# The gated embedding of a two-block transformer forward pass: its product moved to third place in the stream, its gates applied pair by pair, the next stage's chunk splits begun beside it, and the output stored in four parts

## The reference

```python
def swiglu_2(x, wg, wu, wd):
    return (jax.nn.silu(x @ wg) * (x @ wu)) @ wd

for i in range(DEPTH):                       # DEPTH = 2
    x = layer_norm(DN_ALPHA * x + 0.5 * swiglu_2(x, ffn1_wg[i], ffn1_wu[i], ffn1_wd[i]), ...)
    y = mixer_ab(x, ...) if i % 2 == 0 else mixer_c(x, ...)
    x = layer_norm(DN_ALPHA * x + y, ...)
    x = layer_norm(DN_ALPHA * x + 0.5 * swiglu_2(x, ffn2_wg[i], ffn2_wu[i], ffn2_wd[i]), ...)
    x = x + jax.nn.sigmoid(x @ ple_wg[i] + ple_bg[i]) * (p[i] @ ple_wp[i])
return x
```

## Time and profile before

| | |
|---|---|
| median of 3 runs | 2382.51 us |
| the three runs | 2378.83, 2382.51, 2384.23 us |
| profiled execution | 2382.22 us |
| its span in the profile | 2380.4 us |
| TensorE matmuls busy | 2220.4 us (93%) |
| VectorE, ScalarE busy | 1377.1 us (58%), 941.4 us (40%) |
| mean granted clock | 0.967 |

### The profile page before, as it was taken

The page is one execution under the profiler, slowest core; times in us unless marked ns, Lnnn a source line. Parts: engine busy times, 40 slices in busy tenths (PEclk is TensorE's granted clock), DMA queues, the critical chain, the costliest instruction groups (busy, mean ns, idle before and its releaser), DMA issues. The chain is left out here.

```text
span 2380.4 us, 32569 instructions
## 1 busy us (share of the span) xinstructions
PE 2220.4 (93%) x13722; PEld 1897.6 (80%) x13722; DVE 1377.1 (58%) x1600; ACT 941.4 (40%) x1031; POOL 127.0 (5%) x69
## 2 busy tenths in 40 slices
PE   6999889999999978999999979999799998789997
PEld 4887678888888747888888868888788796678886
DVE  4458724756665164666656655655565695636654
ACT  3313323545443143444444443444344444124443
POOL 0056300000000000000000000000000020000000
PEclk8999999999999999999999989999899998899999
DMA  7228804455455301555555414554355442024551
GB/s 313 106 105 358 351 1 152 172 184 182 171 192 182 112 17 71 194 189 183 190 181 193 160 53 150 186 194 159 124 193 182 153 176 73 2 76 154 186 194 54
DMA packets 52481, 373.10 MB, mean 157 GB/s; under 512 B 5728, under 2 KB 6752, under 8 KB 7840
## 3 DMA queue, kind: packets, MB, share of 16 engines
q1 hardware_dynamic: 51584, 367.78, 42.1%
q0 software_dynamic: 800, 3.93, 0.5%
HBM read 370.64 MB, written 1.05 MB: 156 GB/s over the span
## 5 line engine op out<-in xcount | busy, mean ns | idle before, releaser
L359 PE MATMUL PS<-AR_r 128*128 128x512 f32 x2240 | 792.9, 398 | 0.0
L479 DVE TENSOR_TENSOR ring_r<-ring,AR_r 128x2048 fp32r<-128x2048 f32 x270 | 619.1, 2299 | 277.2 <-ACT AR_r L473 277.1
L473 ACT ACTIVATE AR_r<-ring 128x2048 fp32r<-128x2048 f32 x274 | 522.4, 1912 | 315.8 <-PE PS L376 194.0
L360 PE MATMUL PS<-AR_r,ring_r 128*128 128x256 f32 x2240 | 628.2, 280 | 0.0
L359 PEld LDWEIGHTS PS<-AR_r 128*128 128x128 f32 x2240 | 420.8, 188 | 103.1
L360 PEld LDWEIGHTS PS<-AR_r,ring_r 128*128 128x128 f32 x2240 | 422.8, 189 | 2.5
L531 ACT ACTIVATE AR<-PS 128x512 f32<-128x512 f32 x140 | 83.8, 599 | 439.3 <-PE PS L360 439.3
L374 PE MATMUL PS<-AR_r 128*128 128x512 f32 x616 | 242.1, 393 | 0.0
L376 PE MATMUL PS<-AR_r 128*128 128x512 f32 x616 | 240.9, 391 | 0.0
L375 PE MATMUL PS<-ring_r,AR_r 128*128 128x512 f32 x616 | 240.1, 390 | 0.0
L376 PEld LDWEIGHTS PS<-AR_r 128*128 128x128 f32 x616 | 115.6, 188 | 26.3
(11 more groups left out here) (377 smaller groups left out, 3070.2 us busy)
## 6 DMA issues: line engine op xcount, KB each, us to landing
ring<-stream SPq DMA_DIRECT2D x346, 1024.0 KB, 4.8
X<-xt SPq DMA_DIRECT2D x1, 2048.0 KB, 10.1
AR<-bias POOLq DMA_DIRECT2D x1, 1536.0 KB, 6.7
AR<-pt POOLq DMA_DIRECT2D x2, 512.0 KB, 4.3
out<-X SPq DMA_DIRECT2D x1, 1024.0 KB, 4.8
SM<-small SPq DMA_DIRECT2D x1, 545.0 KB, 4.2
AR<-invc SPq DMA_DIRECT2D x1, 512.0 KB, 15.3
X<-negl POOLq DMA_DIRECT2D x1, 512.0 KB, 6.4
```

The source lines that it names most:

```text
L359: pe.matmul(PS[:, bank, :], w_hi, X_PARTS[:, :, k * T:(k + 1) * T], start=(k == 0), stop=False, skip_group_check=True)
L360: ins = pe.matmul(PS[:, bank, 0:T], w_lo, X_HI[:, k, :], start=False, stop=(k == DT - 1), skip_group_check=True)
L473: act.activation(w_hi_of(tag, i), ring[:, n % SLOTS, :], ACT.Identity).then_inc(split_hi, 1)
L479: dve.tensor_tensor(RING_R[:, n % SLOTS, :], ring[:, n % SLOTS, :], w_hi_of(tag, i), ALU.subtract).then_inc(split_lo, 1)
```

## The change

The embedding's chunk becomes a stage of its own (`emb2`, `emb3`) between the first two and the last two gate chunks (`ple2b`, `ple3b`), in the stream and in TensorE's order. VectorE applies pairs 0 and 1 as soon as the embedding's product and their gates are there, pair 2 behind the third chunk's gates, pair 3 behind the fourth's. For layer 2, the splits of ffn4's chunks 0 and 1 are placed between these steps on both engines, and the input's first pair is rounded before the last two gates are taken. ScalarE gets a wait on the last product before that rounding, since `X_HI` is still read until then. The places of the rounded chunks turn differently (`TURN_OF`), and the waits that free them are given by `free`. The output is stored in four transfers, each behind its pair's `ple_out`.

```diff
-          ("ffn2", FF_CHUNKS), ("mix2_in", 7), ("mix2_out", 4), ("ffn3", FF_CHUNKS), ("ple2", 5),
-          ("ffn4", FF_CHUNKS), ("mix3_in", 16), ("mix3_out", 4), ("ffn5", FF_CHUNKS), ("ple3", 5)]
+          ("ffn2", FF_CHUNKS), ("mix2_in", 7), ("mix2_out", 4), ("ffn3", FF_CHUNKS), ("ple2", 2), ("emb2", 1), ("ple2b", 2),
+          ("ffn4", FF_CHUNKS), ("mix3_in", 16), ("mix3_out", 4), ("ffn5", FF_CHUNKS), ("ple3", 2), ("emb3", 1), ("ple3b", 2)]
...
-        TURN_OF = {"ffn1_lat": 2, "ffn2": 2, "mix2_in": 2}
+        TURN_OF = {"ple2b": 2, "ple3b": 2, "ffn4": 1, "mix3_in": 1, "ffn1_lat": 2, "ffn2": 2, "mix2_in": 2}
...
-            act_split_chunk(act, nxt, 2)
+            if nxt.startswith("ple"):
+                act_split_chunk(act, f"{nxt}b", 0, free=START[nxt])
+            else:
+                act_split_chunk(act, nxt, 2)
...
         def pe_ple(pe, l):
-            n0 = START[f"ple{l}"]
             pe_chunks_as_features_come(pe, f"ple{l}", (0, 1), (0, 1))
-            for i in range(2, 4):
-                pe_chunk_split(pe, f"ple{l}", i, i)
-            need_chunk(pe, n0 + 4)
+            n = START[f"emb{l}"]
+            need_chunk(pe, n)
             pe.wait_ge(S["emb_loaded"], S.at("emb_loaded", l))
...
             ins.then_inc(multiplied, 1)
+            for i in range(2):
+                pe_chunk_split(pe, f"ple{l}b", i, 2 + i)
 
         def act_ple(act, order, l):
-            act_split_chunk(act, f"ple{l}", 3)
-            for m in range(DT):
-                need_product(act, START[f"ple{l}"] + m // 2)
-                b = (l - 2) * 8 + m
-                act.activation(SQ[:, m, LAT], ACC[:, m, :], ACT.Sigmoid, bias=sm("ple_bg")[:, b:b + 1]).then_inc(S["ple_gate"], S.mark("ple_gate", (l, m)))
+            first, then = START[f"ple{l}"], START[f"ple{l}b"]
+
+            def gates(q):
+                need_product(act, first + q if q < 2 else then + q - 2)
+                for m in (2 * q, 2 * q + 1):
+                    b = (l - 2) * 8 + m
+                    act.activation(SQ[:, m, LAT], ACC[:, m, :], ACT.Sigmoid, bias=sm("ple_bg")[:, b:b + 1]).then_inc(S["ple_gate"], S.mark("ple_gate", (l, m)))
+
+            def round_up(q):
+                act.wait_ge(S["ple_out"], S.at("ple_out", (l, q)))
+                act.activation(X_HI[:, pair(q), :], XL[:, pair(q), :], ACT.Identity).then_inc(S["x_hi"], S.mark("x_hi", ("ffn4", q)))
+
+            act_split_chunk(act, f"ple{l}b", 1, free=first + 2)
+            for q in range(2):
+                gates(q)
+            if l == 2:
+                act_split_chunk(act, "ffn4", 0, free=first + 2)
+            gates(2)
+            if l == 2:
+                act_split_chunk(act, "ffn4", 1, free=then + 1)
+                act.wait_ge(multiplied, START["ffn4"])
+                round_up(0)
+            gates(3)
+            if l == 2:
+                for q in range(1, GROUPS):
+                    round_up(q)
+                act_split_chunk(act, "ffn4", 2, free=START["ffn4"])
 
         def dve_ple(dve, order, l):
-            dve_split_chunk(dve, f"ple{l}", 3)
-            need_product(dve, START[f"ple{l}"] + 4)
-            dve.wait_ge(S["ple_gate"], S.at("ple_gate", (l, DT - 1)))
             emb = PS[:, 4:8, :].rearrange("p b (m t) -> p (b m) t", t=T)
-            for q in range(GROUPS):
+
+            def add(q):
+                dve.wait_ge(S["ple_gate"], S.at("ple_gate", (l, 2 * q + 1)))
                 dve.tensor_tensor(SQ[:, pair(q), LAT], SQ[:, pair(q), LAT], emb[:, pair(q)], ALU.mult).then_inc(order.sem, order.step())
                 dve.wait_ge(order.sem, order.n)
                 dve.tensor_tensor(XL[:, pair(q)], XL[:, pair(q)], SQ[:, pair(q), LAT], ALU.add).then_inc(S["ple_out"], S.mark("ple_out", (l, q)))
+
+            dve_split_chunk(dve, f"ple{l}b", 1)
+            need_product(dve, START[f"emb{l}"])
+            for q in range(2):
+                add(q)
+            if l == 2:
+                dve_split_chunk(dve, "ffn4", 0)
+            add(2)
+            if l == 2:
+                dve_split_chunk(dve, "ffn4", 1)
+                dve_split_input(dve, "ffn4", XL, (0,))
+            add(3)
+            if l == 2:
+                dve_split_input(dve, "ffn4", XL, (1, 2, 3))
+                dve_split_chunk(dve, "ffn4", 2)
...
-                if l == 3:
-                    dve_split_first(dve, "ffn4")
-                    dve_split_input(dve, "ffn4", XL)
...
-            sp.wait_ge(S["finished"], S.at("finished"))
...
-                sp.dma_start(out, X[:, :, LAT]).then_inc(S["stored"], S.mark("stored", by=16))
+                for q in range(GROUPS):
+                    sp.wait_ge(S["ple_out"], S.at("ple_out", (3, q)))
+                    sp.dma_start(out[:, pair(q), :], XL[:, pair(q), :]).then_inc(S["stored"], S.mark("stored", by=16))
+                sp.wait_ge(S["finished"], S.at("finished"))
...
-                if l == 3:
-                    act_split_first(act, "ffn4")
-                    act_split_input(act, "ffn4", XL, 0, ("ple_out", 2))
```

More of the change, by code:

```diff
@@ L154, in build @@
                 SPLIT_BASE[name] = chunks
-                chunks += 4 if name.startswith("ple") else count
+                chunks += count
         def arena(at, *shape, of=AR):
@@ L1412, in dve_layernorm @@
                     dve_split_input(dve, nxt, XL, (q - 1,))
-            dve_split_chunk(dve, nxt, 2)
+            if nxt.startswith("ple"):
+                dve_split_chunk(dve, f"{nxt}b", 0)
+            else:
+                dve_split_chunk(dve, nxt, 2)
         PEMB = arena(20736, 2, 2, T)
         def pe_ple(pe, l):
-            n0 = START[f"ple{l}"]
             pe_chunks_as_features_come(pe, f"ple{l}", (0, 1), (0, 1))
-            for i in range(2, 4):
-                pe_chunk_split(pe, f"ple{l}", i, i)
-            need_chunk(pe, n0 + 4)
+            n = START[f"emb{l}"]
+            need_chunk(pe, n)
             pe.wait_ge(S["emb_loaded"], S.at("emb_loaded", l))
@@ L1426, in pe_ple @@
                     ins = pe.matmul(PS[:, 4 + m // 2, (m % 2) * T:(m % 2 + 1) * T],
-                                    ring[:, (n0 + 4) % SLOTS, k * D + m * P:k * D + (m + 1) * P], PEMB[:, l - 2, k, :],
+                                    ring[:, n % SLOTS, k * D + m * P:k * D + (m + 1) * P], PEMB[:, l - 2, k, :],
                                     start=(k == 0), stop=(k == 1))
             ins.then_inc(multiplied, 1)
+            for i in range(2):
+                pe_chunk_split(pe, f"ple{l}b", i, 2 + i)
@@ L2092, in build @@
         AFTER = {"mix0": "mix0_out", "layer0": "ffn0_ctx", "mix1": "mix1_out", "layer1": "ffn1_lat", "preffn2": "ffn2",
-                 "mix2": "mix2_out", "layer2": "ple2", "preffn3": "ffn4", "mix3": "mix3_out", "layer3": "ple3"}
+                 "mix2": "mix2_out", "layer2": "ple2b", "preffn3": "ffn4", "mix3": "mix3_out", "layer3": "ple3b"}
         LASTUSE = START[AFTER[stop or "layer3"]] + dict(STAGES)[AFTER[stop or "layer3"]]
@@ L2476, in lay_out @@
         wp = g["ple_wp_2"][l].reshape(2, P, D).transpose(1, 0, 2).reshape(1, P, -1)
-        parts[f"ple{2 + l}"] = np.concatenate([chunks_in(g["ple_wg_2"][l]), wp])
+        wg = chunks_in(g["ple_wg_2"][l])
+        parts[f"ple{2 + l}"], parts[f"emb{2 + l}"], parts[f"ple{2 + l}b"] = wg[:2], wp, wg[2:]
     heads = np.arange(8).reshape(2, 4).T.reshape(-1)
```

## The result

The changed kernel takes 2362.03 us (median of 4 runs, 2361.84 to 2363.24) where the one before takes 2381.59 (median of 4): ratio 0.9919, 95% interval 0.9902 to 0.9936, 19.6 us faster. Two later batches, on two chips, gave 0.9906 (0.9891 to 0.9921) and 0.9916 (0.9901 to 0.9931). The forecast was 2364, with a range of 2361 to 2367.

The account below looks back on a forecast made before the run. TensorE, busy 93% of the span, was taken as the bound, so only its waits and the tail count. 11.3 + 2.0 + 3.1 + 2.2 = 18.6 us off 2382.5 gives 2363.9, said as 2364, range 2361 to 2367.

Parts of the forecast that it names:

- The handover: Layer 2's last product to ffn4's start: a relay of rounding and subtraction, 1.62 us, starts ffn4 11.3 us earlier.
- cover of 1.4 us for chunk 1: Layer 2, VectorE: the low half of ffn4's chunk 1 is done 1.4 us before it is needed, the tightest cover.
- The clock: ffn4's first 96 matmuls: with a short idle gap they run at the upper clock level, 2.0 us faster.
- The tail: Layer 3's end: only two gates and one pair follow the last product, so the last add ends 3.1 us earlier.
- the store: Kernel's end: the last store is 256 KB instead of 1 MB and lands sooner, 2.2 us, bounds 0 and 2.26.
- (a): Rival, chance 0.16: small last store, short gap's clock or chunk 1's low half gives nothing; 2366 to 2370 us.
- (b): Rival, chance 0.04: ffn4 starts early, then waits for weights, so only the tail's gain is left; 2377 us.
- (c): Rival, chance 0.03: shifted work in mixer 3 meets the lower clock level, 45 us more; 2409 us, slower.
- an allowance of 2 us either way: Whole kernel: the clock gate's free-running timing can make the same restart cost differently, 2 us either way.

Follow-up runs that it names:

- e6: The changed kernel with the split of ffn4's chunk 1 moved behind the last product on ScalarE; 2368.95 us, one profiled run.
- e2: The changed kernel with ffn4's chunk splits and its input's rounding all behind layer 2's last pair, as before the change; 2374.05 us.
- e3: The changed kernel with the embedding's product last in both layers, ffn4's three splits still beside it; 2370.07 us.
- e7b: The kernel before with 27 dummy products in TensorE's idle time ahead of ffn4; 2382.11 us beside 2381.77, ratio 1.0001.
- e4: The changed kernel with two dummy roundings on ScalarE ahead of the rounding of ffn4's input; 2362.95 us, one profiled run.
- e1: The changed kernel with one 1 MB store behind the end in place of four; 2365.77 us.
- e8: The changed kernel with layer 2's embedding product for the last two feature tiles moved behind the fourth gate chunk, its chunk last in the stream; 2363.51 us.
- e10: e8 plus, in layer 3, the last gate chunk handed over by feature tile, with a 128 KB store for each; 2363.26 us.
- e5: The changed kernel with six dummy roundings on ScalarE ahead of the rounding of ffn4's input; 2373.91 us, one profiled run.
- e7: The kernel before with 55 dummy products ahead of ffn4, which overran TensorE's idle time; 2388.47 us, one profiled run.

## Why the prediction was right

**The sum (forecast 18.6).** Its four terms measured 19.2 together; C to D gave 0.6 more that nobody forecast, and 0.85 was lost ahead of A, which makes 19.0. The 1.9 us between the forecast of 2364 and the 2362.03 are in part luck of the yardstick: the forecast starts from 2382.51, and the kernel before has a median of 2381.59 with one run more.

**The handover (forecast 11.3, measured 11.4).** Each link came as replayed: the product's end, rounding, low half, start; 1.54 us for 1.62. TensorE's waits for L511 came to 13.7 us, forecast about 14. The cover of 1.4 us for chunk 1 was 1.45. e6 shows that it was needed, and e2 that the place of the splits is most of the gain. The forecast did not separate that from the third place of the product; e3 does, for one order of VectorE's work: in layer 2 the third place is worth 2.0 us of idle time and 1.5 of clock.

**The clock (2.0, measured 2.00).** e7b isolates it, within ffn4's first pair. The argument was weaker than the number, which the short gap might have spoiled: the idle row at clock 1.00 that it rested on was 1.4 us long, and e3 and e4 show that the fall can come after a gap, with the clock at 1.00 all through it. A gap of 1.54 costs nothing, of 3.53 and 3.71 1.5 us, of 5.02 and 8.07 2.5, of 10.15 1.7 and of 12.91 2.0. The cost doesn't grow with the gap: the windows of e6 show the lower level until 5.7 us behind B, those of e2, with the longer gap, until 4.0 us.

**The tail (3.1, measured 3.12), the store (2.2, measured 2.71).** The store is the term that was mis-sized, past its own bound of 2.26, which only counted bytes at 348 GB/s; each of the four stores landed after 2.1 to 2.2 us, where the last was to take 2.5 to 3.1. The windows of both kernels at 0.2 us give the rest: bytes flow for some 0.8 us instead of 3.0 (2.25), they start about 0.9 us after the issue begins instead of 1.3 (0.4), and the issue itself stands 0.03 us behind the last add instead of 0.15, since no memset lies between (0.1). e1 confirms the whole at 2.7. The Trainium skill's figures (DMA: Bandwidth & Descriptors, Anatomy of one DMA) gave an estimate of 2.6 us for the small store; they are fitted there to transfers that GpSimd issues, and the trace has 2.1 for this one of SyncE's.

**The rivals.** (a): none of its parts occurred; of these the short gap's clock had the least to go by. (b): no matmul behind ffn4's start waited for the stream. (c): mixer 3's slow stretch moved with the kernel and cost nothing more (C to D 0.6 shorter). But the mechanism exists in small: e7b, e8 and e10 each lose 1.5 us at the next layernorm for the 1.7 to 2.0 won before it. That the changed kernel is spared this was not foreseen; the forecast only had an allowance of 2 us either way.

**What stays open.** The layernorm gap keeps the clock in the changed kernel and loses it in e8, though its work and the length of its first wait are the same. The profiles show that the distance from A is what differs. In all fourteen the clock, at its lower level just before A, is back at 1.00 between 0.1 and 0.4 us before it. In the six kernels whose gap before B costs clock it falls 33.8 to 34.2 us behind A, whatever the gap's length: in e3 and e4 that is right behind the gap's end, in the kernel before, e2, e5 and e6 inside it. In the kernel before:

```profile
1672.40:1675.90 3.50, 0.00 (x0) 0.00 (x0) 3.40 (x6) 3.46 (x2) 0.00 (x0) 1.00 0.69 241
1676.20:1685.20 9.00, 0.00 (x0) 0.00 (x0) 8.93 (x8) 5.32 (x7) 0.00 (x0) 0.50 0.02 9
```

The changed kernel's gap is over 31.7 us behind A, so these runs do not tell whether its length or its place saves it. At ffn4's layernorm the clock stays up with A to C of 43.3 (changed), 46.8, 47.0, 53.6 and 56.7 us, and falls with 41.6 (e8, e10), 49.3 (e6), 52.4 (e5), 54.7 (e7b) and 65.3 (e7): neither early nor late is safe. In e5 and e6 it is up again when TensorE restarts behind the gap (1874.48 in e6), and their C to D is 640.3 and 640.6 us beside 639.8 to 640.1 in the changed kernel and e1 to e4; in e7, e7b, e8 and e10 the lower level lies behind the restart (1868.50 in e8). First e6, then e8:

```profile
1872.00:1874.48 2.48, 1.82 (x10) 1.45 (x8) 2.48 (x6) 1.26 (x2) 0.00 (x0) 0.57 0.17 73
1874.48:1879.00 4.52, 4.52 (x38) 4.52 (x39) 3.56 (x7) 2.85 (x3) 0.00 (x0) 1.00 0.00 0
```

```profile
1864.00:1868.50 4.50, 3.15 (x17) 2.58 (x17) 4.50 (x9) 2.04 (x3) 0.00 (x0) 0.65 0.48 200
1868.50:1872.00 3.50, 3.50 (x16) 3.50 (x17) 3.30 (x7) 1.83 (x3) 0.00 (x0) 0.50 0.00 0
```

The Trainium skill (TensorE: Matmul & The Clock Gate, Part 1) calls the gate's timing free-running; the spread of A, 1639.23 to 1644.30 over profiles that do the same work ahead of it (1638.66 with e7), agrees with that. That the falls stand at like distances from A, also in e8 and e10, whose A differs by 2.2 us, fits that the loss recurs over whole batches (e8's five runs have a mean granted clock of 0.969 or 0.970, all but one of the changed kernel's twelve 0.971 or 0.972). That the distance from A is the cause is argued from these profiles: no run moved the layernorm and nothing else.

## What to carry to other kernels

When a stage's inputs are handed over through several engines, list what stands in series behind the last product and ask of each item whether it needs that product: here three weight splits did not, two were moved ahead of it and one behind the input's halves, and that was worth 10 of 19 us, while the reordering of TensorE's own work was worth some 6, about half of it in each layer. Then check the order on each in-order engine by its tightest cover; a single chunk split (1.9 us on ScalarE, then 2.3 on VectorE) behind the wait gave 6 us back, 2.5 of them through the clock. Measure such edits by stretches between fixed events of a profile, and look at the stretches that nobody touched too.

## What was not expected of the hardware

The granted clock can fall after a short gap is over: 1.00 during 3.53 us of idle time, 0.51 for the 2.8 us of full work behind it. A local gain can be paid back far away: 1.72 us won before ffn4, 1.5 lost behind its layernorm, 190 us later, and in the kernel before 2.0 won and 1.5 lost in the same places. And halving a store from 256 to 128 KB took only 0.2 us off its landing (2.1 to 1.9), where going from 1 MB to 256 KB had taken 2.7 (4.8 to 2.1).
